# Recurrence stage: token tiles in halves, stores on GpSimd's queue, head and weight loads spread over units

## What is computed

```python
x = layer_norm(x, ln_in_g, ln_in_b)
h = x @ w_in                                   # 1024 -> 6144
q_na, k_na, v_na, q_hg, z_f, z_b, i_hg, g_hg, gate_na, gate_hg = split(h)
a_out = neighbourhood_attention(q_na, k_na, v_na, rpb) @ w_branch_na
o_hg = hgrn2_bidirectional(silu(q_hg), i_hg, z_f, z_b, lb_f, lb_b)   # 4 heads of 128
r_out = (rms_norm_heads(o_hg, g) * silu(g_hg)) @ w_branch_hg
mix = sigmoid(gate_na) * a_out + sigmoid(gate_hg) * r_out
x = layer_norm(ALPHA * x + mix @ w_out, ln1_g, ln1_b)
y = expert_choice_ffn(x, w_router, w_gate, w_up, w_down)             # 16 experts
x = layer_norm(ALPHA * x + y, ln2_g, ln2_b)
```

## Time and profile before

| | us |
|---|---|
| timed runs (3) | 2669.75, 2670.01, 2675.24 |
| median | 2670.01 |
| profiled execution, span | 2678.6 |
| TensorE busy in it | 2608.3 (97%) |
| VectorE, ScalarE, GpSimd busy | 1668.0, 1370.1, 391.8 |
| recurrence in the trace | from about 567 to 880 |

### The profile page before, as it was taken

One profiled execution on the slowest core, in us unless ns is written; L12 is line 12 of the kernel. 1 busy time (PEld: TensorE's weight loads), 2 busy tenths in 40 slices (PEclk: granted clock), 3 DMA queues, 4 the chain that ended last, 5 costly groups with the idle time before them and its releaser, 6 DMA issues.

```text
span 2678.6 us, 44950 instructions
## 1 busy us (share of the span) xinstructions
PE 2608.3 (97%) x18524; PEld 2063.9 (77%) x18524; DVE 1668.0 (62%) x2127; ACT 1370.1 (51%) x1808; POOL 391.8 (15%) x422
## 2 busy tenths in 40 slices
PE   9999999999999999969999999999999999999997
PEld 7888888778877788757777777777777777777676
DVE  7212230876554566677766777667776677767788
ACT  3111220876653433425665566656666566656674
POOL 2211120000000244310010011001100110011344
PEclk9999999999999999989999999999999999999999
DMA  7567783687656744367887788878788778888983
GB/s 252 174 198 209 241 275 133 222 303 263 238 190 241 254 142 154 114 230 277 303 287 292 280 301 285 310 277 296 285 298 304 279 287 308 312 288 324 327 317 137
DMA packets 238347, 683.59 MB, mean 255 GB/s; under 512 B 20081, under 2 KB 66680, under 8 KB 233024
## 3 DMA queue, kind: packets, MB, share of 16 engines
q1 hardware_dynamic: 220608, 630.58, 65.1%
q0 software_dynamic: 17536, 50.14, 6.7%
HBM read 576.67 MB, written 103.95 MB: 254 GB/s over the span
## 4 chain that ended last, share of the span: by engine, by line
PE 53%; DMA 1%; POOL 1%; DVE 1%; issue 0%; ACT 0%; ACTq 0%; POOLq 0%; DVEq 0%
PE moe_strip L2683 12%; PE moe_down L2698 4%; PE moe_up L2698 4%; PE moe_down L2700 4%; PE moe_down L2699 4%; PE moe_up L2699 4%; PE moe_gate L2698 4%; PE moe_up L2700 4%; PE moe_gate L2700 4%; PE moe_gate L2699 4%; DMA out<-moe_norm_x 1%; PE moe_up L2620 1%; PE moe_turn L2656 1%; POOL moe_minus_mean L2502 0%; PE moe_gate L2631 0%
## 5 line engine op out<-in xcount | busy, mean ns | idle before, releaser
L2914 DVE TENSOR_TENSOR pieces_low<-pieces_raw,pieces_high 128x1024 fp32r<-128x1024 f32 x768 | 893.8, 1219 | 348.6 <-PE moe_strip L2683 335.2
L2806 ACT ACTIVATE pieces_high<-pieces_raw 128x1024 fp32r<-128x1024 f32 x768 | 769.0, 1051 | 340.0 <-PE moe_up L2700 202.6
L2683 PE MATMUL moe_strip<-pieces_raw,pieces_xT_p 128*32 128x256 f32 x4096 | 227.9, 380 | 0.5 <-ACT pieces_xT_p L2818 0.5
L2698 PE MATMUL moe_up<-pieces_high,pieces_xT 128*128 128x512 f32 x512 | 204.0, 398 | 4.9 <-DVE pieces_low L2914 4.9
L2698 PE MATMUL moe_gate<-pieces_high,pieces_xT 128*128 128x512 f32 x512 | 202.4, 395 | 0.7 <-DVE pieces_xT L2919 0.7
L2698 PE MATMUL moe_down<-pieces_high,pieces_hdn 128*128 128x512 f32 x512 | 202.7, 396 | 0.0
L2683 PEld LDWEIGHTS moe_strip<-pieces_raw,pieces_xT_p 128*32 128x32 f32 x4096 | 129.7, 110 | 93.8 <-issue 10.9
L2699 PE MATMUL moe_up<-pieces_high,pieces_xT 128*128 128x512 f32 x512 | 200.5, 392 | 0.0
L2700 PE MATMUL moe_up<-pieces_low,pieces_xT 128*128 128x512 f32 x512 | 199.9, 390 | 0.0
L2700 PE MATMUL moe_gate<-pieces_low,pieces_xT 128*128 128x512 f32 x512 | 199.6, 390 | 0.0
L2700 PE MATMUL moe_down<-pieces_low,pieces_hdn 128*128 128x512 f32 x512 | 199.5, 390 | 0.0
(11 more groups left out here) (393 smaller groups left out, 5198.4 us busy)
## 6 DMA issues: line engine op xcount, KB each, us to landing
pieces_raw<-in_w_gate_e SPq DMA_DIRECT2D x128, 1024.0 KB, 5.8
pieces_raw<-in_w_up_e SPq DMA_DIRECT2D x128, 1024.0 KB, 7.3
pieces_raw<-in_w_down_e SPq DMA_DIRECT2D x128, 1024.0 KB, 5.0
bias_fx<-xs SPq DMA_DIRECT2D x40, 1024.0 KB, 5.3
fr_raw<-in_w_in SPq DMA_DIRECT2D x16, 1024.0 KB, 8.2
ws<-fr_late_split SPq DMA_DIRECT2D x32, 512.0 KB, 4.3
bias_fw<-ws SPq DMA_DIRECT2D x32, 512.0 KB, 9.0
mo_gates<-h SPq DMA_DIRECT2D x20, 512.0 KB, 4.5
```

Source lines behind the costliest of these rows:

```text
L2683: last = nc.tensor.matmul(strip_ps[j * CP:(j + 1) * CP, kind, :], x, raw[g % RAW][:, k * D + j * STRIP:k * D + (j + 1) * STRIP], start=sta ...
L2698: nc.tensor.matmul(to[:], x_k[:, kk, 0:CS], hi, start=(kk == 0), stop=False)
L2806: nc.scalar.activation(high[:, g % HI, cols], raw[g % RAW][:, cols], ACT.Copy).then_inc(hi_done, 1)
L2914: nc.vector.tensor_tensor(low[g % RAW][:, cols], raw[g % RAW][:, cols], high[:, g % HI, cols].bitcast(F32), ALU.subtract).then_inc(lo_done, 1)
```

## The change

SyncE's order in the recurrence is made anew. A token tile comes as two halves of 512 KB, each with its own semaphore, and each half is issued as soon as TensorE has read the same half of the tile two units before. TensorE waits for each half at its own start. The stores of units and of head outputs go from SyncE's queue to GpSimd's. The loads of heads 2 and 3 stand behind the token tile of the head's first unit (k), of its second (q) and of its third (v). Mixing's first five weights go one per unit behind the tokens of units 28 to 32. In mixing the tiles come by halves too; the stores stay with SyncE there, on semaphores of their own.

```diff
+        begin_at = [units_until((hd - 1, "added")) for hd in range(HG_HEADS)]
...
-                def load_tile(i):
-                    sp.wait_ge(fx_half, 2 * (i - 1))
-                    sp.dma_start(fx[:, i % 2].bitcast(F32), xs[i % NT]).then_inc(fx_in[i % 2], 16)
...
+                def load_half(i, half):
+                    sp.wait_ge(fx_half, 2 * (i - 2) + half + 1)
+                    ks = slice(4 * half, 4 * half + 4)
+                    sp.dma_start(fx[:, i % 2, :, ks, :].bitcast(F32), xs[i % NT, :, :, ks, :])\
+                      .then_inc(fx_in[2 * (i % 2) + half], 16)
...
                 for i in range(HERE):
-                    if i in heads_begin:
-                        store_head(heads_begin[i] - 1)
-                        if heads_begin[i] + 1 < HG_HEADS:
-                            load_head(heads_begin[i] + 1)
-                        else:
-                            sp.wait_ge(o_mm, (HG_HEADS - 1) * NG)
-                            load_first_weights(sp)
                     new_slab = i % NT == NT - 1 and i // NT + 1 < len(LATER)
...
-                    if i + 2 < U:
-                        load_tile(i + 2)
+                    for half in range(2):
+                        load_half(i + 2, half)
...
-                    store_unit(i)
                     if 1 <= i <= 4:
                         load_head(1, (i - 1,))
-                store_head(HG_HEADS - 1)
+                    for hd in range(2, HG_HEADS):
+                        if 0 <= i - begin_at[hd - 1] < 3:
+                            load_head(hd, ((0, 1), (2,), (3,))[i - begin_at[hd - 1]])
+                    if 0 <= i - begin_at[HG_HEADS - 1] < SLOTS:
+                        if i == begin_at[HG_HEADS - 1]:
+                            sp.wait_ge(o_mm, (HG_HEADS - 1) * NG)
+                        load_first_weight(sp, i - begin_at[HG_HEADS - 1])
...
             @block.gpsimd
...
+                for i in range(HERE):
+                    if i in begin_at[1:]:
+                        store_head(begin_at.index(i) - 1)
+                    store_unit(i)
+                store_head(HG_HEADS - 1)
...
-                    if half == 0:
-                        pe.wait_ge(fx_in[i % 2], 16 * (i // 2) + 16)
-                        if i >= 2:
-                            pe.wait_ge(f_copied, i - 1)
+                    pe.wait_ge(fx_in[2 * (i % 2) + half], 16 * (i // 2) + 16)
+                    if half == 0 and i >= 2:
+                        pe.wait_ge(f_copied, i - 1)
```

More of the change, by code:

```diff
@@ L1106, in _, with store_unit, store_head @@
                       .then_inc(iota_done, 1)
+                def store_unit(i):
+                    pool.wait_ge(f_copied, i + 1)
+                    at = LATER[i // NT] * SLAB
+                    pool.dma_start(h[i % NT * P:(i % NT + 1) * P, at:at + SLAB], fout[i % 2])\
+                        .then_inc(f_stored[i % 2], 16)
+                def store_head(hd):
+                    pool.wait_ge(o_copied, (hd + 1) * NG)
+                    pool.dma_start(o[:, hd * P:(hd + 1) * P].rearrange("(t p) c -> p t c", p=P), chunked(A))\
+                        .then_inc(o_stored, 16)
+                for i in range(HERE):
[3 more added lines that the diff above has]
+                store_head(HG_HEADS - 1)
             @block.tensor
@@ L1516, in stage_mix_out @@
     U = len(LATER) * NT
+    HERE = U - TAIL
     fw, fx, fw_in, fx_in, fx_half, f_copied, f_stored = filling
@@ L1714, in _ @@
                         for u in range(2):
-                            sp.wait_ge(f_stored[u], 16 * (U // 2))
+                            sp.wait_ge(f_stored[u], 16 * (HERE // 2))
+                            sp.wait_ge(f_stored[2 + u], 16 * (TAIL // 2))
                         sp.wait_ge(w_lo_done, BLOCKS)
@@ L1798, in fill @@
                 def fill(i):
-                    pe.wait_ge(fx_in[i % 2], 16 * (i // 2) + 16)
                     pe.wait_ge(f_copied, i - 1)
                     for c in range(KD):
+                        if c % 4 == 0:
+                            pe.wait_ge(fx_in[2 * (i % 2) + c // 4], 16 * (i // 2) + 16)
                         n = i // NT * KD + c
@@ L1895, in evict @@
                     act.wait_ge(fx_half, 2 * i + 2)
-                    act.wait_ge(f_stored[i % 2], 16 * (i // 2))
+                    act.wait_ge(f_stored[i % 2], 16 * (HERE // 2))
+                    if i >= HERE + 2:
+                        act.wait_ge(f_stored[2 + i % 2], 16 * ((i - HERE) // 2))
                     nc.scalar.activation(fout[i % 2], acc_out[i % 2][:], ACT.Copy).then_inc(f_copied, 1)
@@ L1903, in weight_hi @@
                         for u in range(2):
-                            act.wait_ge(f_stored[u], 16 * ((U - TAIL) // 2))
+                            act.wait_ge(f_stored[u], 16 * (HERE // 2))
                     if n == 2 * KB:
@@ L3141, in build @@
             fw_in, fx_in = ([nc.alloc_semaphore(f"fill_{name}{n}") for n in range(count)]
-                            for name, count in (("fw_in", KRING), ("fx_in", 2)))
+                            for name, count in (("fw_in", KRING), ("fx_in", 4)))
             fx_half, f_copied, o_stored = (nc.alloc_semaphore(f"fill_{name}") for name in ("half", "copied", "o_stored"))
-            f_stored = [nc.alloc_semaphore(f"fill_stored{n}") for n in range(2)]
+            f_stored = [nc.alloc_semaphore(f"fill_stored{n}") for n in range(4)]
             filling = (fw, fx, fw_in, fx_in, fx_half, f_copied, f_stored)
@@ L3148, in load_filler @@
                 for i in range(2):
-                    sp.dma_start(fx[:, i].bitcast(F32), xs[i]).then_inc(fx_in[i], 16)
+                    for half in range(2):
+                        ks = slice(4 * half, 4 * half + 4)
+                        sp.dma_start(fx[:, i, :, ks, :].bitcast(F32), xs[i, :, :, ks, :])\
+                          .then_inc(fx_in[2 * i + half], 16)
                 for n in range(KRING):
@@ L3172, in build, with load_first_weight @@
             w_in_room = [nc.alloc_semaphore(f"mo_w_ready{n}") for n in range(SLOTS)]
[L3174 to L3178, removed]
+            def load_first_weight(sp, n):
+                src = (w_na, w_hg)[n * P // NAW]
+                sp.dma_start(wroom[:, n * D:(n + 1) * D], src[n * P % NAW:n * P % NAW + P, :])\
+                  .then_inc(w_in_room[n], 16)
             stage_recurrence(nc, ident, h, hT, xs, ws, lb, lb_in, o, table[:],
-                             wroom[:], filling, o_stored, head_in, aT_stored, load_first_weights)
+                             wroom[:], filling, o_stored, head_in, aT_stored, load_first_weight)
         gates = [s.sb(f"gates{n}", [CAPS[n], NE]) for n in range(2)]
```

14 lines of the change are left out of this document (2 added, 12 removed).

## The result

The changed kernel took 2678.8 us at the median of 13 runs, the kernel before 2672.8 us at the median of 13 on the same chip: a ratio of 1.0027, 95% interval 1.0020 to 1.0034. It is slower: by 6.0 us in the medians and 7.2 us by the ratio, of which the interval leaves 5.3 to 9.1; forecast were 9.8 us less. The profiled execution has a span of 2677.0 us, 1.6 us shorter than that of before, and that hides the loss. The difference between the spans comes from outside the change.

The account below looks back on a forecast made before the run. It took TensorE, 97% busy, as the bound, with time to regain only in its idle or low-clock spans. 7.0 + 2.9 - 2.6 - 1.0 + 3.5 = 9.8 us less than 2670.0 gave 2660.2 us, range 2652 to 2673.

Parts of the forecast that it names:

- rivals with chances of .08 and .11: Recurrence's end: barrier waits for GpSimd's store, 2665.1 us (0.08). Heads: late k makes ScalarE the bound, 2667.6 us (0.11).
- a third of .12: Rival at mixing's start: mixing gives nothing, its chain being bound elsewhere; 6.3 us less gain, 2663.7 us; chance 0.12.
- The stall of head 2: Recurrence, head 2: a token tile late behind 2.6 MB of loads; wait and low clock go, 7.0 us gained.
- The stall of head 3: Recurrence, head 3: mixing weights ahead of tiles and weight blocks; spreading them gains 2.9 us, low end 1.5.
- k late: Heads 1 and 2: later-issued k lands after 7.4 us, delaying ScalarE's eviction; TensorE stalls 1.3 us each, cost 2.6.
- both ends: Bounds of k's cost: 0 if it lands in 5.3 us, 5 us per head if 3 us later with low clock.
- The barrier: Between recurrence and mixing: GpSimd issues the last head's output more slowly, cost 1.0 us, bounds 0.3 and 5.9.
- its rival: Barrier before mixing is held until GpSimd's store lands: 5.9 instead of 1.0 us, 2665.1 us; chance 0.08.
- Mixing's start: Earlier first half tile lets o arrive sooner; waits and low clock shrink, 3.5 us gained.
- The term's best end: Best case for mixing's start: waits shrink and the low clock goes, given as 4.6 us; worst 0.
- The stores of the units: Recurrence: unit stores on GpSimd's queue stay hidden, cost 0, with about 14 us to land.
- The slower rival: Last head's output lands after 21.8 us, delaying mixing: 2675.5 us, or 2682.9 with the ScalarE rival; chance 0.09.

Follow-up runs that it names:

- E2: Changed kernel with k issued ahead of its unit's token halves, q and v each one unit earlier; 2669.5 us, ratio .9988 to the kernel before.
- E3: Changed kernel with k ahead of the tokens as in E2 and the last head's output on SyncE's queue; 2663.2 us, .9967 of the kernel before.
- E11: Kernel before with only the head loads and mixing weights spread over units, whole tiles, stores on SyncE's queue; 2678.0 us, ratio 1.0023.
- E7: Kernel before with only the token tiles split in halves; loads, weights and stores as they were; 2663.0 us, ratio .9967.
- E6: E3 with mixing's five weights moved from units 28 to 32 to units 31 to 35; 2664.1 us, .9970 of the kernel before.
- E4: Changed kernel with only 64 KB of the last head's output on GpSimd's queue, the other 576 KB on SyncE's; 2678.4 us, one run.
- E5: Kernel before with only the recurrence's stores moved to GpSimd's queue; 2680.0 us, ratio 1.0026.
- E9: E3 with both halves of a token tile issued at the end of the unit; 2665.7 us, .9978 of the kernel before.
- E1: Changed kernel with the last head's output back on SyncE's queue; 2673.2 us, 1.0004 of the kernel before.
- E8: E3 with mixing's first head output o loaded between the halves of its first token tile; 2660.5 us, .9958 of the kernel before.
- E10: E7 with mixing's first head output o loaded between the halves of its first token tile; 2660.6 us, .9956 of the kernel before.

## Why the prediction was wrong

It had each mechanism that decided, two of them as rivals with chances of .08 and .11 and a third of .12, and put its own sum on none of them. All three came true together: 9.8 less, less 7.4, less 4.9, less 3.5 is 6.0 slower, beside 7.2 measured. That this comes so near is partly luck: head 3 gave 2.2 us less than this sum has, and mixing, which has nothing in it, gave 1.45.

- *The stall of head 2, 7.0 us.* Right: head 2 is back to 68.9 in E2 and E3. But there are two cures, and I counted one. I gave the gain to the 2.6 MB leaving the line, and E11 shows that this does remove the wait; E7 still has them in the line and gains 5 of the 7 us with the halves alone.
- *The stall of head 3, 2.9 us.* 0.7 came. I took all of it for mixing's weights in the line; E6, with these weights out of the way, gains another 0.75, and 0.9 of the 1.2 us left are waits for a weight block and a half tile.
- *k late, 2.6 us: the first step that failed.* The chain was right link by link (late k, 7.25 us to the eviction, no free accumulator), its start was not. I had k issued at the end of the unit and landing 7.4 us later, a sum and not a row. It went out 0.57 us after that end, since the issue of the second half stands ahead of it (0.6 us, at 669.07 to 669.64), and was opened 8.7 and 9.1 us after its issue. These 1.9 and 2.3 us went in full into the pause: 3.31 and 3.70 instead of 1.3. Then came what follows a pause, the lower clock or a wait for VectorE, 1.9 and 1.35 us. Sum 10.2 against 2.6. Why the landing took 1.3 and 1.7 us more than the sum has was not tested. In head 1 two transfers ran beside it that the sum left out, the next half tile (issued at 671.80, 2.2 us behind k) and GpSimd's store of a unit (669.98); at 366 GB/s their 0.79 MB would take 2.1 us, an estimate. E2, which moves only k and with it q and v, gives the whole back in the heads: 10.2 us, and 10.4 by the two ratios. A stall that is a difference of two long times was worth no more than the error of either; I had both ends in hand (0 and 5 us a head) and chose near the low one because "its terms are all measured", while the landing was not.
- *The barrier, 1.0 us: the second step that failed.* 5.8 us of wait, 5.5 in the stage. The upper bound of the prediction, 5.9, was the truth, and it was also the price of its rival. E4 and E5 show that the landing decides (E6 and E9 show it with a unit's store), E1 that a SyncE store in the same place costs nothing (2.8 us of wait, as before). The trace held no open GpSimd transfer at any barrier, and I took that silence for a low price.
- *Mixing's start, 3.5 us: the third.* 1.45 came, and not from o's wait: that was 1.8 instead of 1.9 and the lower clock came after it (matmuls of 0.63 us from 909.9 on). The first half does leave the line ahead of o, and o lands 4.35 us after its issue instead of 5.05. But o is issued 8.5 us after mixing's first matmul instead of 7.65: the second half ahead of it starts at 895.76, 0.36 us later than the whole tile did (the first unit took longer, with 10 matmuls in its first 4 us at a clock of 0.50, where before had 11 at 0.59), its issue takes 0.52 us instead of 0.33, and o follows 0.34 us behind that. Both effects cancel. What had to move was o, which E8 and E10 do. (The term's best end adds to 4.7 and not 4.6, which changes nothing.)
- *The stores of the units* cost nothing in after, as forecast: they land 3.7 and 4.6 us after their issue at the median of the two buffers and 8.4 at most, with 14 us to spare. The last one is nearer to its limit: it is issued some 5 us before the stage ends, and in E6 and E9 it held the barrier. The slower rival, a head's output of 1280 pieces landing after 21.8 us, was far off: 4.4 us.

The Trainium skill, page "DMA: Bandwidth & Descriptors", section "Measured (HBM→SBUF, 128 partitions, SWDGE, issued from GpSimd)", advises batches of 1 MiB or more. The page's fit, for transfers issued from GpSimd, made two half tiles 2 us dearer than one whole in the prediction's estimate; the tiles here are SyncE's. The rows have 4.3 us for a half and 5.3 for a whole tile, and E7, in which only the size changes, with its signals and the earlier issue of the first half, is 9 us faster. Here the advice did not carry. Whether the smaller piece or its earlier issue brings this was not taken apart: E9, without the early issue, keeps 0.22% of the 0.33%, but with the loads spread.

## What to carry to other kernels

Before a transfer on GpSimd's queue is put at the end of a stage, ask what barrier follows: give the last store to another queue, and leave on it only those that end well before: the landing and 3.2 us more must fit in front of the barrier, which for the last unit's store failed in E6 and E9. When loads are spread behind others, first give each its latest start (need, less landing in a full queue), and move only those with room; here k had none. Splitting a buffer in two with a signal each was the simplest part of this change and by the times all of its gain; try the parts of a bundle alone before you keep the bundle.

## What the hardware showed that I had not expected

- The barrier between two stages stays closed until a transfer on GpSimd's own queue has landed, and 3.2 us more, for 64, 256 and 640 KB alike (E4; E6 and E9; after and E5). TensorE waited 7.6 us there with 64 KB open and 8.6 with 640 (2.8 when SyncE's queue does the store, which is then still open: issued at 878.72, it lands 3.6 us later, and mixing's first matmul is at 881.03). The DRAIN that GpSimd issues there is itself recorded with 34 to 52 ns, so it is in the idle time before the next instruction that the wait shows.
- GpSimd needs 0.97 us to issue a store of 1280 pieces of 512 B, 0.54 for one of 128 rows of 2 KB and also for one of 128 pieces of 512 B.
- The length of a pause alone does not tell whether the lower clock follows. In mixing, ahead of the first turned output, pauses of 1.8 to 2.7 us were followed by it (before, after, E2, E5, E7, E9, E11); of those of 1.6 and 1.7 us, the ones in E4 (1.7) and E6 (1.6) were and the ones in E1 (1.6) and E3 (1.7) were not; after 0.3 us (E8, E10) it stayed at full speed. In the recurrence of after, 3.31 us were followed by it and 3.70 were not. At the start of mixing, behind the barrier, TensorE ran its first 4 us at a mean of 0.50 to 0.63 in twelve of the fourteen traces and at full speed in two, E1 and E10, which are also the two with the shortest mixing. E10's first 4 us of mixing, columns as in the earlier trace rows, have 18 matmuls at full clock; before had 11 in them, at a mean of 0.59:

```profile
871.72:875.72 4.00, 4.00 (x18) 3.31 (x19) 3.23 (x5) 3.98 (x5) 0.47 (x2) 1.00 0.90 255
```

What makes the difference stays open. By the count of matmuls (7 of 0.23 us) it is worth 1.6 of the 4 us by which mixing differs between E10 and E7, an estimate.
